# Attention of a hybrid decoder layer: from one head at a time to pairs of heads on the two halves of the array

## The reference

```python
h = rmsnorm(x, g_mix[l]); proj = h @ w_in[l]
# branch A, per head (SEQ = 256 is one block): causal softmax with ALiBi
s_own = einsum('bhqd,bhkd->bhqk', qx, k_own) * scale - slopes * d_own      # masked to k <= q
y = softmax(s_own) @ v
# branch B, per head: stick breaking
z = einsum('bhqd,bhkd->bhqk', qx, kx) * scale
sp = where(causal, softplus(z), 0.0)
log_rest = cumsum(sp, axis=3, reverse=True) - sp
a = where(causal, exp(log_sigmoid(z) - log_rest), 0.0); y = a @ vx
# merge
x = x + (sigmoid(gate_a) * (y_a @ w_br_moba) + sigmoid(gate_b) * (y_b @ w_br_sb)) @ w_out
x = x + cross_attention(rmsnorm(x), rmsnorm(mem), ...)
x = x + square(relu(rmsnorm(x) @ w_up)) @ w_down;  return rmsnorm(x, g_final)
```

## Time and profile before

| | |
|---|---|
| device time, median of 3 runs | 451.23 us (449.95 to 452.59) |
| span of the profiled execution | 449.3 us |
| time around the span (median less span) | 1.9 us |
| TensorE busy | 438.3 us, 98% of the span |
| TensorE weight loads busy | 400.4 us, 89% |
| VectorE busy | 271.3 us, 60% |
| ScalarE busy | 213.4 us, 47% |
| mean granted TensorE clock | 0.994 |

### The profile page before, as it was taken

One profiled execution on the slowest core, in us unless ns is written; L12 is line 12 of the kernel. 1 busy time (PEld: TensorE's weight loads), 2 busy tenths in 40 slices (PEclk: granted clock), 3 DMA queues, 4 the chain that ended last, 5 costly groups with the idle time before them and its releaser, 6 DMA issues.

```text
span 449.3 us, 6925 instructions
## 1 busy us (share of the span) xinstructions
PE 438.3 (98%) x2884; PEld 400.4 (89%) x2884; DVE 271.3 (60%) x340; ACT 213.4 (47%) x268; POOL 25.1 (6%) x39
## 2 busy tenths in 40 slices
PE   6999999999999999999999999999999999999993
PEld 6999988989998999988998889999999999999982
DVE  4769556866666534886567867655555555555525
ACT  5753338755545471382527654444444444444413
POOL 0079000000000000000020000000000000000001
PEclk9899999999999999999999999999999999999999
DMA  7998554333322235455443335555555555556002
GB/s 228 415 420 342 188 187 171 112 103 128 136 104 95 94 137 179 171 206 202 144 182 140 116 119 188 188 188 187 188 187 188 189 187 187 187 187 233 0 0 93
DMA packets 12970, 77.46 MB, mean 172 GB/s; under 512 B 1552, under 2 KB 2064, under 8 KB 4496
## 3 DMA queue, kind: packets, MB, share of 16 engines
q1 hardware_dynamic: 12800, 77.08, 46.9%
q10 hardware_dynamic: 144, 0.02, 0.0%
HBM read 76.04 MB, written 1.05 MB: 172 GB/s over the span
## 4 chain that ended last, share of the span: by engine, by line
PE 95%; DVE 1%; DMA 1%; ACT 1%; SPq 0%; issue 0%; POOLq 0%; POOL 0%; DVEq 0%; ACTq 0%
PE bank L856 41%; PE bank L875 33%; PE bank L971 11%; PE bank L1007 2%; DMA xT_raw<-in_xT_dram 1%; PE bank L1053 1%; PE bank L1008 1%; PE bank L929 1%; PE bank L1073 1%; PE bank L934 1%; PE bank L928 1%; PE bank L889 1%; DVE res L808 1%; PE bank L989 1%; PE bank L940 1%; DVE xs L814 0%
## 5 line engine op out<-in xcount | busy, mean ns | idle before, releaser
L554 DVE TENSOR_TENSOR w_lo<-raw,w_hi 128x2048 fp32r<-128x2048 f32 (+3 forms) x76 | 155.4, 2069 | 43.0 <-ACT w_hi L363 41.6
L363 ACT ACTIVATE w_hi<-raw 128x2048 fp32r<-128x2048 f32 x65 | 122.3, 1909 | 36.0 <-PE bank L856 19.4
L856 PE MATMUL bank<-hT_hi,w_hi 128*128 128x256 f32 x416 | 119.4, 287 | 2.9 <-DVE w_lo L554 2.4
L856 PE MATMUL bank<-hT_lo,w_hi 128*128 128x256 f32 x416 | 118.8, 286 | 0.0
L856 PE MATMUL bank<-hT_hi,w_lo 128*128 128x256 f32 x416 | 118.8, 286 | 0.0
L856 PEld LDWEIGHTS bank<-hT_hi,w_hi 128*128 128x128 f32 x416 | 81.0, 195 | 4.2 <-DVE hT_lo L576 2.6
L856 PEld LDWEIGHTS bank<-hT_lo,w_hi 128*128 128x128 f32 x416 | 81.0, 195 | 0.6
L856 PEld LDWEIGHTS bank<-hT_hi,w_lo 128*128 128x128 f32 x416 | 81.0, 195 | 0.0
L510 ACT ACTIVATE relu<-bank 128x512 f32<-128x512 f32 x16 | 9.6, 598 | 95.7 <-PE bank L856 95.7
L777 DVE TENSOR_TENSOR relu<-relu 128x512 f32<-128x512 f32 x16 | 11.1, 693 | 61.6 <-ACT relu L510 61.6
L875 PE MATMUL bank<-w_hi,aT_hi 128*128 128x512 f32 x144 | 46.0, 392 | 0.0
(11 more groups left out here) (156 smaller groups left out, 610.8 us busy)
## 6 DMA issues: line engine op xcount, KB each, us to landing
raw<-in_weights_dram SPq DMA_DIRECT2D x65, 1024.0 KB, 4.8
raw<-in_weights_dram SPq DMA_DIRECT2D x7, 256.0 KB, 6.3
raw<-in_weights_dram SPq DMA_DIRECT2D x2, 512.0 KB, 7.8
res<-in_x_dram SPq DMA_DIRECT2D x2, 512.0 KB, 11.9
mem_tok<-in_mem_dram SPq DMA_DIRECT2D x1, 1024.0 KB, 9.6
memT_raw<-in_memT_dram SPq DMA_DIRECT2D x1, 1024.0 KB, 8.3
out_dram<-xs SPq DMA_DIRECT2D x2, 512.0 KB, 2.6
xT_raw<-in_xT_dram SPq DMA_DIRECT2D x3, 256.0 KB, 5.5
```

Of the source, the lines that this page charges most:

```text
L363: copy(w_hi[:, slot, :], raw[:, rslot, :], ACT.Copy).then_inc(w_hi_ready, 1)
L554: return nc.vector.tensor_tensor(dst, whole, high.bitcast(fp32), sub)
L856: last = mm(outs[m], w, v[:, k0 + k, :], start=first and n == 0, stop=k == nk - 1 and n == 2, skip_group_check=bool(kt_wait))
```

## The change

Two heads, an even and an odd one, become one step (p = 0 to 3) on every engine.

- **TensorE.** `scores(p)` issues each score product for the even head (partitions 0 to 63) and then for the odd head (64 to 127), kind by kind, each head into a bank of its own; then the two masks. `attended(p)` does the same with the value products: even head into partitions 0 to 63, odd into 64 to 127, both branches in one bank (7). The number of products is as before. The loop's order for a pair is: all of gate chunk 2p, sums of both heads, six transposes, first half of gate chunk 2p + 1, `scores(p + 1)`, second half, `attended(p)`.
- The sums use a float32r `neg_ones_r` on `sp_hi` and on `sp_lo` in place of fp32 `neg_ones` on `sb_sp`: two MATMULs for a head, as before.
- **ScalarE and VectorE.** Abs, Exp, Ln, `sp_hi`, the final Exp, `sb_sp`, `sp_lo`, `aT_hi` and `aT_lo` work on two heads in one instruction. The four maxima, softmax exponentials, normalizations of a pair stay one by one. The order of splits, evacuations and outputs in their loops is rewritten.
- **Waits.** The logits' banks now serve every pair, not every other head: `scores(p + 1)` waits for `sb_exp` and `mo_pt` of pair p. Bank 3 holds both the odd head's scores and its transposes. The memory norm's broadcast is moved to just ahead of gate chunk 0, into bank 1, and its copy on VectorE behind the split of chunk 15; TensorE waits for that copy (`row_ready`) ahead of gate chunk 1.

In the diff below, removed lines that stand in the functions printed above are left out where a body is rewritten.

```diff
         sb_aT = sb("sb_aT", [P, 2, 384])
-        sb_t = sb("sb_t", [P, 384])
-        sb_sp = sb("sb_sp", [P, 384])
-        sp_hi = sb("sp_hi", [P, 384], f32r)
-        sp_lo = sb("sp_lo", [P, 384], f32r)
+        sb_t, o_t = place("sb_t", [P, 2, 384])
+        sp_hi = sb("sp_hi", [P, 2, 384], f32r, over=o_t)
+        sb_sp, o_sp = place("sb_sp", [P, 2, 384])
+        sp_lo = sb("sp_lo", [P, 2, 384], f32r, over=o_sp)
         gated_a = sb("gated_a", [P, 2, 512], over=o)
         gated_b = sb("gated_b", [P, 2, 512], over=o + 4096)
...
+        neg_ones = neg_ones_r[:, :].bitcast(fp32)
         ident_r = sb("ident_r", [P, P], f32r)
         neg_tri_r = sb("neg_tri_r", [P, P], f32r)
         future_r = sb("future_r", [P, 2, P], f32r)
...
+        MO_S, MO_PT, SB_Z, ATT_O = (2, 3), (6, 3), (4, 5), 7
         WARM_UP = 8
         V_BANKS, MV_BANKS, X_S, X_PT = ((0, 1), (6, 7)), (5, 2), (0, 1, 3, 6), (7, 4, 3, 6)
-        X_ROW_BANK, MEM_ROW_BANK = 7, 3
+        X_ROW_BANK, MEM_ROW_BANK = 7, 1
         x_in = [sem(f"x_in{t}") for t in range(TOK)]
...
@@ -406,28 +408,29 @@
             def att_high(p):
...
+                act.wait_ge(sb_av, p + 1)
+                copy(aT_hi[:, p:p + 5:4, :], bank[ATT_O].rearrange("p (b q) -> p b q", b=2), ACT.Copy)\
+                    .then_inc(att_hi, 1)
+            def softplus_exp(p):
+                act.wait_ge(sb_z, p + 1)
+                if p:
+                    act.wait_ge(sb_c, p)
+                copy(sb_t[:, :, :], banks[:, SB_Z[0]:SB_Z[1] + 1, 0:384], ACT.Abs).then_inc(sb_abs, 1)
+                act.wait_ge(sb_abs, p + 1)
+                copy(sb_t[:, :, :], sb_t[:, :, :], ACT.Exp, scale=-1.0).then_inc(sb_e, 1)
+                act.wait_ge(sb_e, p + 1)
+                copy(sb_t[:, :, :], sb_t[:, :, :], ACT.Ln, bias=1.0).then_inc(sb_ln, 1)
+                act.wait_ge(mo_biased, p + 1)
+                for i in range(2):
+                    for q, (a, b) in enumerate(((0, 128), (128, 384))):
+                        last = copy(mo_u[:, i, a:b], mo_u[:, i, a:b], ACT.Exp,
+                                    bias=mo_nmax[:, 2 * i + q:2 * i + q + 1],
+                                    accum_out=mo_sum[:, 2 * i + q:2 * i + q + 1])
                 last.then_inc(mo_exp, 1)
...
+                act.wait_ge(sb_raw, p + 1)
+                copy(sp_hi[:, :, :], sb_sp[:, :, :], ACT.Copy).then_inc(sp_hi_done, 1)
             act.wait_ge(memT_in, 16)
             split(12)
...
...
+            for p in range(HEADS // 2):
+                act.wait_ge(sb_c, p + 1)
+                if p:
+                    act.wait_ge(sb_av, p)
+                copy(sb_aT[:, :, :], banks[:, SB_Z[0]:SB_Z[1] + 1, 0:384], ACT.Exp).then_inc(sb_exp, 1)
+                split(GATE0 + 2 * p + 4)
+                if p + 1 < HEADS // 2:
+                    softplus_exp(p + 1)
+                att_high(p)
+                split(GATE0 + 2 * p + 5)
             act.wait_ge(gate_evac, 8)
...
@@ -626,60 +629,69 @@
             last.then_inc(sumsq_dve, 1)
             def att_low(p):
...
+                dve.wait_ge(att_hi, p + 1)
+                low(aT_lo[:, p:p + 5:4, :], bank[ATT_O].rearrange("p (b q) -> p b q", b=2), aT_hi[:, p:p + 5:4, :])\
+                    .then_inc(att_lo, 1)
+            def scores(p):
+                dve.wait_ge(mo_s, p + 1)
+                if p:
+                    dve.wait_ge(mo_t, p)
+                for i in range(2):
+                    for q, (a, b, c) in enumerate(((0, 128, 128), (128, 384, 0))):
+                        last = nc.vector.tensor_tensor_reduce(out=mo_u[:, i, a:b], in0=bank[MO_S[i]][:, a:b],
+                                                              in1=alibi[:, 2 * p + i, c:SEQ], scale=1.0, scalar=-3e38,
+                                                              op0=ALU.add, op1=ALU.max,
+                                                              accum_out=mo_max[:, 2 * i + q:2 * i + q + 1])
                 step(last)
                 nc.vector.tensor_scalar(mo_nmax[:, :], mo_max[:, :], -1.0, None, ALU.mult).then_inc(mo_biased, 1)
...
+                dve.wait_ge(sb_ln, p + 1)
+                nc.vector.scalar_tensor_tensor(sb_sp[:, :, :], banks[:, SB_Z[0]:SB_Z[1] + 1, 0:384], 0.0, sb_t[:, :, :],
                                                ALU.max, ALU.add).then_inc(sb_raw, 1)
...
+                dve.wait_ge(mo_exp, p + 1)
                 step(nc.vector.reciprocal(mo_rsum[:, :], mo_sum[:, :]))
...
+                for i in range(2):
+                    for q, (a, b) in enumerate(((0, 128), (128, 384))):
+                        last = nc.vector.tensor_scalar(mo_u[:, i, a:b], mo_u[:, i, a:b],
+                                                       mo_rsum[:, 2 * i + q:2 * i + q + 1], None, ALU.mult)
                 last.then_inc(mo_normed, 1)
...
+                dve.wait_ge(sp_hi_done, p + 1)
+                low(sp_lo[:, :, :], sb_sp[:, :, :], sp_hi[:, :, :]).then_inc(sp_lo_done, 1)
             dve.wait_ge(alibi_ready, HEADS)
             scores(0)
             diagonal(MEM, 2)
             split(13)
...
             for k in range(KT):
                 low_in(MEM, k, mT_hi, mT_lo, memT_raw, G_MEM)
                 if k == KT // 2:
                     split(14)
             split(15)
...
+            spread(mem_row, MEM_ROW_BANK, 2)
+            def gate_out(h):
                 dve.wait_ge(w_used, GATE0 + h + 1)
                 nc.vector.tensor_tensor(flat(gateT[:, 2 * h:2 * h + 2, :]), bank[h % 2][:, :],
                                         flat(rstd_row[:, :, :]), ALU.mult).then_inc(gate_evac, 1)
...
+            dve.wait_ge(lo_done[MEM], KT)
+            for p in range(HEADS // 2):
+                gate_out(2 * p)
+                dve.wait_ge(mo_t, p + 1)
+                if p:
+                    dve.wait_ge(sb_av, p)
+                for i in range(2):
+                    last = nc.vector.tensor_copy(mo_pT[:, i, :], bank[MO_PT[i]][:, 0:384])
+                last.then_inc(mo_pt, 1)
+                split(GATE0 + 2 * p + 4)
+                if p + 1 < HEADS // 2:
+                    scores(p + 1)
+                gate_out(2 * p + 1)
+                att_low(p)
+                split(GATE0 + 2 * p + 5)
             split(24)
             def mem_k_out(i, b):
...
@@ -918,27 +930,34 @@
                           pieces_of(c) if c <= 2 else None,
                           (lambda: spread_rstd(X_ROW_BANK, 1)) if c == 3 else None)
...
+            def scores(p):
+                if p:
+                    pe.wait_ge(mo_pt, p)
+                    pe.wait_ge(sb_exp, p)
+                heads = [(i, slice(DH * i, DH * i + DH)) for i in range(2)]
+                for i, r in heads:
+                    q, k = qkT[r, p, :], qkT[r, 4 + p, :]
+                    mm(bank[MO_S[i]][:, 0:128], q[:, 0:P], k[:, 0:P], start=True, stop=True)
+                for i, r in heads:
+                    q, k = qkT[r, p, :], qkT[r, 4 + p, :]
+                    last = mm(bank[MO_S[i]][:, 128:384], q[:, P:SEQ], k, start=True, stop=True)
+                last.then_inc(mo_s, 1)
+                for i, r in heads:
+                    q, k = qkT[r, 8 + p, :], qkT[r, 12 + p, :]
+                    mm(bank[SB_Z[i]][:, 0:256], k[:, 0:P], q, start=True, stop=False, skip_group_check=True)
+                for i, r in heads:
+                    q, k = qkT[r, 8 + p, :], qkT[r, 12 + p, :]
+                    mm(bank[SB_Z[i]][:, 256:384], k[:, P:SEQ], q[:, P:SEQ], start=False, stop=False,
+                       skip_group_check=True)
+                if p == 0:
                     pe.wait_ge(masks_ready, 2)
...
+                for i in range(2):
+                    last = mm(bank[SB_Z[i]][:, 0:384].rearrange("p (b q) -> p b q", b=3)[:, 0:3:2, :], ident_r[:, :],
+                              future_r[:, :, :], start=False, stop=False, skip_group_check=True)
+                last.then_inc(sb_z, 1)
             for c in range(8, 12):
...
+            def gate(h, m):
+                c = GATE0 + h
+                for kk in range(KT):
+                    a = kk * 256 + m * P
+                    wh, wl = w_hi[:, c % RING, a:a + P], w_lo[:, c % RAW, a:a + P]
+                    for n, (w, v) in enumerate(((wh, hT_hi), (wh, hT_lo), (wl, hT_hi))):
+                        last = mm(halves(h % 2)[m], w, v[:, kk, :], start=kk == 0 and n == 0,
+                                  stop=kk == KT - 1 and n == 2)
+                return last
+            def attended(p):
+                o = bank[ATT_O]
+                for b, a_ in enumerate((mo_pT, sb_aT)):
+                    if b == 1:
+                        pe.wait_ge(sb_exp, p + 1)
+                    for kt, (qa, qb, ka, kb) in enumerate(((0, 256, 0, 256), (128, 256, 256, 384))):
+                        for i in range(2):
+                            v0 = b * WIDTH + DH * (2 * p + i)
+                            last = mm(o[DH * i:DH * i + DH, SEQ * b + qa:SEQ * b + qb], v_tok[:, kt, v0:v0 + DH],
```

(66 more changed lines are left out.)

94 lines of the change are left out of this document (9 added, 85 removed).

## The result

The changed kernel takes 439.12 us (median; 438.04 to 439.82, 4 runs) against 450.71 us of the kernel before beside it: a ratio of 0.9731, with a 95% interval of 0.9705 to 0.9757. That is 11.6 us less; 441.2 was predicted, inside the range of 438.5 to 448.5.

A forecast was written before the change was run, and what follows sets the result against it. TensorE was taken to bound the kernel. Savings of 2.8 and 7.5 us less a 0.3 us wait gave 10.0 us off the 449.3 us span, so 439.3, or 441.2 us as median; range 438.5 to 448.5.

The forecast's parts named there:

- Term 1: Around score and value products on TensorE: pairing heads halves the changes of array shape, 0.18 us each, saving 2.8 us.
- Term 2: Score and value products: the odd head's run on the other half beside the even head's, saving 7.5 us.
- the layout in units: Score and value blocks counted in 0.107 us steps: 16 and 15 of them, against 24 each without overlap.
- rival D: Score and value blocks: each product hides fully beside its partner, halving every block; 438.5 us, chance 0.08.
- The two signs with numbers: In TensorE's timeline: the pair's period falls from 20.2 to some 17.6 us; its score block to mask takes 2.3 us.
- A: Whole kernel: the terms as summed, with partial overlap of the halves worth 7.5 us; 441.2 us, chance 0.40.
- B: Score and value products: weight loads for the other half wait their turn, overlap worth 5.0 us; 443.7 us, chance 0.22.
- C: Score and value products: no overlap, only the saved changes of shape count; 448.4 us, chance 0.17.
- E: Score and value blocks: each alternation between halves costs 0.18 us, 10.0 us in all; 458.4 us, chance 0.07.
- Term 3: Sums, transposes, masks, gate matmuls, moved broadcast and wider evacuations: costs cancel, 0, at most 0.1 us for the sums.
- Term 4: New waits: the pair's longer softplus chain stays covered, cost 0; TensorE waits 0.3 us for the norm's copy before the loop.
- F: Sums of a pair: the softplus chain is not covered, TensorE waits 3.3 us at three pairs; 451 us, chance 0.06.

The follow-up runs named there:

- same_half: Changed kernel with the odd head's score and value products put on the even head's half of the array, so nothing overlaps; 449.2 us.
- kinds_apart: Changed kernel with the kinds of product of six score and value blocks spread between gate matmuls, 36 more changes of array shape; 445.0 us.
- chain5: Changed kernel with five extra unread ScalarE copies in the softplus chain of pairs 1 to 3; 438.5 us.
- chain13: Changed kernel with thirteen extra unread ScalarE copies in the softplus chain of pairs 1 to 3; 460.6 us.
- norm_first: Changed kernel with VectorE's copy of the memory norm moved ahead of the split of chunk 15; 438.2 us.

## Why the prediction was right, point by point

**Term 1, changes of shape, 2.8 us: right.** same_half keeps this, the new wait (0.4 us in its trace too) and the wider instructions of the other engines: 2.5 us less than before, and 2.5 + 0.4 of wait is 2.9. kinds_apart prices a change at 0.18 us.

**Term 2, the two halves at once, 7.5 us: right in kind, too small.** It measured 10.5 us (the stretches of same_half and the changed kernel), 5.3 in the scores and 5.2 in the value products. What failed is the layout in units: "only the second even one can run beside the first odd one", starts in order, and 16 weight loads "one after the other". In fact the odd head's first pass starts with the even head's first, past the even one's second pass, and loads of the two halves run side by side. That is rival D (chance 0.08), and its 10.4 us are the measured size. The two signs with numbers speak for D as well. The score block was to take 2.3 us in A, which is its 1.71 with both changes (0.38) and both masks (0.24); counted so, it takes 1.9 (from 109.56 + 0.12 to 111.62). The pair's period was to be 17.6 us, and it is 16.9, which is 20.2 less 0.7 of changes and 2.6 of overlap. So A, for which 441.2 was given, isn't what happened; the measured time is in the range because the range reached down to D's 438.5. My argument that the other half has no running product in its way was sound for loads, and I should have followed it to the products too. B and C priced the overlap at 5.0 and 0, and same_half finds 10.5. E wanted 458.4: alternating between halves costs nothing that shows, as four MATMULs on two halves take the time of two on one.

**Term 3, nothing: right.** The sums of a head take 0.58 us as before (105.00 to 105.58 in the changed kernel's timeline, from L1012 of the even head to L1012 of the odd one).

**Term 4, waits: right.** The chain was 6.4 us (at most 7.5 predicted), the cover 3.6 (3): from the start of the chain to the sums it was 10.1 us and not the 10.6 counted, and the chain was shorter by more. chain5 and chain13 show both sides of the cover, so F falls. The wait for the norm was put at 0.3 us; the row has 0.4 and norm_first wins 0.4 by removing it.

**Sum.** 2.9 + 10.5 - 0.4 = 13.0 against a stretch that is 12.9 us shorter. The 11.6 us of the medians are 1.3 less. That this is the front of the kernel is likely but not shown for the medians: there the two profiles differ by 1.1 us, and over all traces the first score product starts between 65.8 and 69.0 us. In spans the forecast was 439.3 and the measurement 437.5: 1.8 less, which is 2.9 in the stretch less the 1.1 of the front.

## What to carry to other kernels

Where products use half of the array's rows or columns, put neighbours on opposite halves: here the second half was free for fp32 in both directions, worth 2.6 us for a pair of heads (10.5 us in all), 3.6 times as much as the saved changes of shape. Alternate finely, for TensorE passed over one waiting product but not two or three. Gather what has one shape, as each change costs 0.18 us; and check the serial chain on the other engines against TensorE's work that covers it, because an uncovered wait of 5.1 us brought the low clock as well, which cost another 2.1 us each time.

## What the runs showed of the hardware

- Two fp32 products on opposite halves, next to each other in the list, start about 0.01 us apart and take the time of one: four MATMULs in 0.49 us against two in 0.48; their weight loads too, four in 0.30 us against two in 0.29.
- Matmuls may start out of list order: L941 of the odd head at 109.87, ahead of L947 of the even head at 110.30, which stands before it.
- A change of the array's shape cost 0.18 us (36 more cost 6.5 us), a direct one from 128*64 to 64*128 no more; fp32 after float32r in the same shape cost nothing (0.12 us from start to start).
- During waits of 5.1 us the granted clock fell to the half level, and it stayed there for 4.5, 4.3 and 4.2 us after TensorE went on.
